# Feed-forward stage on the un-normalized residual, factors applied at eviction; retention scores first; last column's half on VectorE

## The reference

```python
def rms_norm(x, w):
    y = x * lax.rsqrt(jnp.mean(x * x, axis=-1, keepdims=True) + EPS)
    return y * w

h = h + mixed @ w_out                      # 1024 -> 1024
hn = rms_norm(h, ffn_norm_w)
gate, up = jnp.split(hn @ w_gate_up, 2, axis=-1)      # 2 x 2816
h = h + (jax.nn.silu(gate) * up) @ w_down             # 2816 -> 1024
x = rms_norm(h, final_norm_w)
```

## Time and profile before

| | us |
|---|---|
| median of 3 runs | 1132.07 (1131.16 to 1133.46) |
| profiled execution | 1132.3 |
| its span (first to last instruction) | 1130.4 |
| PE busy | 1022.8 (90%) |
| PE loading weights | 712.6 (63%) |
| DVE busy | 845.2 (75%) |
| ACT busy | 423.5 (37%) |
| POOL busy | 305.3 (27%) |
| mean granted clock of TensorE | 0.971 |

### The profile page before, as it was taken

How to read it: one execution, slowest core, us unless ns; L and a number is a source line. 1 busy time by engine, 2 the same in 40 slices (tenths; PEclk the granted TensorE clock), 3 DMA queues, 4 the chain that set the end, 5 groups by cost and what they waited for, 6 DMA issues and landing times.

```text
span 1130.4 us, 14392 instructions
## 1 busy us (share of the span) xinstructions
PE 1022.8 (90%) x5138; PEld 712.6 (63%) x5138; DVE 845.2 (75%) x1758; ACT 423.5 (37%) x842; POOL 305.3 (27%) x288
## 2 busy tenths in 40 slices
PE   7999999999999999999999998878868777777897
PEld 7999999999998877976665554333323333232342
DVE  6979799989778994686796776686776677677555
ACT  7636544354466654352332231221222222122122
POOL 0300000000000000245555534444434444444340
PEclk9999999999999999999999999898989999989899
DMA  9642479898918334599999999999999999999995
GB/s 358 226 149 94 150 281 370 300 333 325 314 55 341 132 115 160 223 420 420 422 420 422 421 422 421 422 422 421 421 422 421 422 420 422 422 421 421 421 422 208
DMA packets 68183, 378.61 MB, mean 335 GB/s; under 512 B 7568, under 2 KB 7952, under 8 KB 35600
## 3 DMA queue, kind: packets, MB, share of 16 engines
q0 software_dynamic: 37152, 268.45, 57.2%
q1 hardware_dynamic: 29808, 106.09, 25.9%
q10 hardware_dynamic: 1152, 3.15, 0.8%
HBM read 376.61 MB, written 1.05 MB: 334 GB/s over the span
## 4 chain that ended last, share of the span: by engine, by line
PE 53%; DMA 32%; DVE 9%; ACT 3%; issue 2%; POOL 1%; POOLq 0%; DVEq 0%; ACTq 0%
DMA ring_sb<-in_peer,idsb 13%; DMA whi_rows<-in_peer,idsb 10%; PE pb L445 9%; PE pb L448 9%; PE pb L954 8%; PE pb L957 7%; PE pb L473 5%; DMA x_rows<-in_peer,idsb 3%; DMA xn<-in_peer,idsb 3%; DMA whi_rows<-in_peer,halves 3%; PE pb L908 2%; PE pb L669 2%; DVE ring_lo L1502 2%; PE pb L894 2%; PE pb L833 1%
## 5 line engine op out<-in xcount | busy, mean ns | idle before, releaser
L2196 DVE CUSTOM_DVE_ANT_0 ring_sb<-ring_sb,arena 128x1024 f32<-128x1024 f32 x127 | 155.2, 1223 | 67.9 <-DMA ring_sb<-in_peer,idsb 67.1
L2319 POOL DMA_INDIRECT ring_sb<-in_peer,idsb x126 | 145.4, 1154 | 144.2 <-PE pb L957 123.5
L445 PE MATMUL pb<-xhi,whi 128*128 128x256 f32 x704 | 178.7, 289 | 4.0 <-DVE arena L1930 2.0
L448 PE MATMUL pb<-xlo,whi 128*128 128x256 f32 x704 | 175.2, 284 | 0.2
L1428 ACT ACTIVATE arena<-arena 128x4 f32<-128x4 f32 (+2 forms) x77 | 15.8, 205 | 425.4 <-DVE arena L2196 425.4
L954 PE MATMUL pb<-ring_sb,arena 128*128 128x512 f32 x254 | 137.5, 624 | 36.2 <-ACT arena L1433 36.2
L2319 POOL DMA_INDIRECT arena<-in_peer,idsb x36 | 40.3, 1119 | 461.3 <-DVE idsb L2087 421.4
L1502 DVE TENSOR_TENSOR ring_lo<-ring_sb,whi 128x1024 fp32r<-128x1024 f32 x126 | 147.8, 1219 | 11.9 <-ACT whi L1017 11.9
L445 PEld LDWEIGHTS pb<-xhi,whi 128*128 128x128 f32 x704 | 135.0, 192 | 7.9 <-issue 2.7
L448 PEld LDWEIGHTS pb<-xlo,whi 128*128 128x128 f32 x704 | 135.0, 192 | 2.4 <-issue 1.4
L957 PE MATMUL pb<-ring_sb,arena 128*128 128x512 f32 x254 | 134.3, 611 | 0.0
(11 more groups left out here) (408 smaller groups left out, 1865.8 us busy)
## 6 DMA issues: line engine op xcount, KB each, us to landing
ring_sb<-in_ada SPq DMA_DIRECT2D x48, 512.0 KB, 5.4
ring_sb<-in_w_gu SPq DMA_DIRECT2D x44, 512.0 KB, 6.9
ring_sb<-in_w_in SPq DMA_DIRECT2D x38, 512.0 KB, 8.2
ring_sb<-in_w_down SPq DMA_DIRECT2D x22, 512.0 KB, 6.0
ring_sb<-in_w_out SPq DMA_DIRECT2D x16, 512.0 KB, 3.5
ring_sb<-in_w_q SPq DMA_DIRECT2D x8, 512.0 KB, 3.9
whi_rows<-in_w_q SPq DMA_DIRECT2D x6, 512.0 KB, 8.7
ring_sb<-in_w_iv SPq DMA_DIRECT2D x4, 512.0 KB, 17.3
```

What stands on the lines that cost most here:

```text
L445: e.matmul(o, hi_w(u)[:, c], xh(k), start=start, stop=False, skip_group_check=skip)
L448: e.matmul(o, hi_w(u)[:, c], xl(k), start=False, stop=False, skip_group_check=skip)
L2196: e.tensor_tensor_reduce(o, o, h2t[tile], 1.0, 0.0, MUL, ADD, aa[:, col:col + 1]).then_inc(*VD.up(("dot", col)))
L2319: e.indirect_dma_start(rows_at[s], None, peer, bass.IndirectOffsetOnAxis(ap=idsb[:, col:col + 1], axis=0)).then_inc(s_row[s], 16)
```

## The change

- *Un-normalized input.* The feed-forward products take h x gain in place of h x gain x rstd. High parts (`ffn_hi`, ScalarE, with the gain as scale) and remainders (`ffn_lo`, VectorE) are written during the output projection, four tiles into places of `xhi`/`xlo` that are free then (`fhi_of(k)` is tile (k+4) mod 8), four after its last product. `normed("n1")` and `x_hi("n1")` go.
- *TensorE's start.* Gate/up 0 is computed in two halves over the feature tiles (`gemm_halves`), with the sums of squares between them and no filler products.
- *Factors at eviction.* In each of the 22 steps VectorE waits for gate/up j and multiplies both halves by the tokens' factors out of PSUM into one SBUF buffer `gus` (`scaled`, 128x512). Sigmoid, silu and glu read `gus`. `sgm` has two buffers in place of four.
- *Order on VectorE.* Within a step the ada parts stand between `scaled` and silu, where they stood behind the rest of glu. The rotary angles move behind the first `scaled`.
- *ScalarE's order.* The two split units that `take` gave at the end of the projection are split behind the last `ffn_hi`, one on each side of `root`/`inv_root`.
- *Scores first.* `scale_x1` moves behind `ret_scores` 0 to 3, and the two group norms behind the scores of their groups.
- *Last column.* For column 255, TensorE adds only the second half of the up row. VectorE adds the first half in `finish`, by a multiplication with the weight and an addition of PSUM.

```diff
+        fhi_of = lambda k: one_(xhi, (k + 4) % 8)
+        flo_of = lambda k: one_(xlo, (k + 4) % 8)
...
-        sgm = [arena[:, i * T:(i + 1) * T] for i in range(4)]
+        gus, sgm = arena[:, 0:2 * T], [arena[:, i * T:(i + 1) * T] for i in (2, 3)]
...
+            def gemm_halves(us, name, until, of, mid):
+                b = bank(until)
+                where[name] = b
+                for h in range(2):
+                    for i, u in enumerate(us):
+                        o = one_(pb[b], i)
+                        if h == 0:
+                            e.wait_ge(*HI.at(u))
+                        for k in range(4 * h, 4 * h + 4):
+                            product(o, u, kc(k), k, fhi_of, flo_of, k == 0 and i == 0, True, (of, k) if i == 0 else False)
+                        if h == 0:
+                            e.wait_ge(*rest_of(u))
+                        for k in range(4 * h, 4 * h + 4):
+                            mm = e.matmul(o, lo_w(u)[:, kc(k)], fhi_of(k), start=False, stop=k == KD - 1, skip_group_check=True)
+                        if h:
+                            mm.then_inc(*USED.up(u))
+                    if h == 0:
+                        mid()
...
-            sums("n1", (4, 10), (AN, ("n1", "ln")))
...
-                gemm([U_gate[j], U_up[j]], ("gu", j), (VG, ("glu", j)), fresh="n1" if j == 0 else None)
+                if j == 0:
+                    gemm_halves([U_gate[0], U_up[0]], ("gu", 0), (VG, ("gu", 0)), "n1", lambda: sums("n1", (0, 0), (AN, ("n1", "ln"))))
+                else:
+                    gemm([U_gate[j], U_up[j]], ("gu", j), (VG, ("gu", j)), xh=fhi_of, xl=flo_of)
...
+                    first_end = end if tile == 0 else col == 254
...
-                    mm = e.matmul(pb[4 + 2 * tile][:, :], dgr[col % 8], o[:, 1024:1536], start=begin, stop=end)
-                    if end:
-                        mm.then_inc(*PU.up(("half", tile)))
+                    if col < 255:
+                        mm = e.matmul(pb[4 + 2 * tile][:, :], dgr[col % 8], o[:, 1024:1536], start=begin, stop=first_end)
+                        if first_end:
+                            mm.then_inc(*PU.up(("half", tile)))
...
+                    if name == "wo":
+                        la.used(2)
+                        if i == 3:
+                            e.wait_ge(*USED.at(us[3][1]))
+                            ffn_hi(4)
+                            ffn_hi(5)
+                        for k in (2 * i, 2 * i + 1):
+                            e.wait_ge(*VN.at((name, k)))
+                            square("n1", k)
+                        if i < 2:
+                            ffn_hi(2 * i)
+                            ffn_hi(2 * i + 1)
+                        if i == 3:
+                            ffn_hi(6)
+                            ffn_hi(7)
+                            rest = new
...
+            def ffn_hi(k):
+                e.activation(fhi_of(k), hk(k), ACT.Copy, scale=vc("ffn", k)).then_inc(*XHI.up(("n1", k)))
...
-            residual(U_wo, "wo", hg_norm)
+            first = residual(U_wo, "wo", hg_norm)
+            split(first[0:1])
             root("n1")
             inv_root("n1")
-            x_hi("n1")
+            split(first[1:2])
...
-                    s = sgm[j % 4]
-                    e.wait_ge(*USED.at(U_up[j]))
-                    if j >= 4:
-                        e.wait_ge(*GLO.at(j - 4))
-                        e.wait_ge(*GHI.at(j - 4))
-                    e.activation(s, one_(pb[where["gu", j]], 0), ACT.Sigmoid).then_inc(*AG.up(("sg", j)))
+                    s = sgm[j % 2]
+                    e.wait_ge(*VG.at(("gu", j)))
+                    if j >= 2:
+                        e.wait_ge(*GLO.at(j - 2))
+                        e.wait_ge(*GHI.at(j - 2))
+                    e.activation(s, one_(gus, 0), ACT.Sigmoid).then_inc(*AG.up(("sg", j)))
...
+                    if name == "wo" and i in (0, 1, 3):
+                        for k in (2 * i, 2 * i + 1) if i < 2 else range(4, 8):
+                            ffn_lo(k)
                     split(la.fill() if i < 2 else new)
+
+            def ffn_lo(k):
+                e.wait_ge(*XHI.at(("n1", k)))
+                e.scalar_tensor_tensor(out=flo_of(k), in0=hk(k), scalar=vc("ffn", k), in1=fhi_of(k).bitcast(F32), op0=MUL,
+                                       op1=SUB).then_inc(*XLO.up(("n1", k)))
...
-            normed("n1", lambda k: vc("ffn", k), one_(rstd, 0))
...
-                    s, b = sgm[j % 4], where["gu", j]
-                    e.wait_ge(*AG.at(("sg", j)))
-                    e.tensor_tensor(s, one_(pb[b], 0), s, MUL).then_inc(*VG.up(("silu", j)))
-                    e.wait_ge(*VG.at(("silu", j)))
-                    e.tensor_tensor(s, s, one_(pb[b], 1), MUL).then_inc(*VG.up(("glu", j)))
-                    e.wait_ge(*GHI.at(j))
-                    e.tensor_tensor(al_of(j), s, ah_of(j).bitcast(F32), SUB).then_inc(*GLO.up(j))
+                    s = sgm[j % 2]
+                    if j == 0:
+                        e.wait_ge(*AN.at(("n1", "rstd")))
+                    e.wait_ge(*USED.at(U_up[j]))
+                    scaled(gus, where["gu", j], VG, ("gu", j))
+                if j == 0:
+                    angles()
                 for n_ in ada_at[j]:
                     if n_ < 46:
                         ada_part(n_)
                     if n_ == 23:
                         turn_32(0)
                         sums_of_32(0)
+                if j < NF:
+                    e.wait_ge(*AG.at(("sg", j)))
+                    e.tensor_tensor(s, one_(gus, 0), s, MUL).then_inc(*VG.up(("silu", j)))
+                    e.wait_ge(*VG.at(("silu", j)))
+                    e.tensor_tensor(s, s, one_(gus, 1), MUL).then_inc(*VG.up(("glu", j)))
+                    e.wait_ge(*GHI.at(j))
+                    e.tensor_tensor(al_of(j), s, ah_of(j).bitcast(F32), SUB).then_inc(*GLO.up(j))
                 if 2 <= j < NF:
                     take([U_dn[j - 2]], 1)
...
-            scale_x1()
...
             for h in range(4):
                 ret_scores(h)
-                if h == 2:
-                    group_rms(("o", 0), vc("sbo"), half(ys, 0))
+            scale_x1()
+            group_rms(("o", 0), vc("sbo"), half(ys, 0))
             take(U_rg[0:2])
-            group_rms(("o", 1), vc("sbo"), half(ys, 1))
             for h in range(4, 8):
                 ret_scores(h)
+            group_rms(("o", 1), vc("sbo"), half(ys, 1))
...
+                    if tile and g == 0:
+                        e.wait_ge(*VD.at(("act", NB - 1)))
+                        e.wait_ge(s_up[1], 16)
+                        e.scalar_tensor_tensor(out=dg[:, gsl], in0=rows_at[row_of[255][0]][:, 1024:1536], scalar=ae[:, 255:256],
+                                               in1=pb[6][:, :], op0=MUL, op1=ADD).then_inc(*VO.up("last row"))
+                        e.wait_ge(*VO.at("last row"))
+                        e.tensor_tensor(dg[:, gsl], dg[:, gsl], g2b[:, gsl], MUL).then_inc(*VO.up((tile, g)))
```

More of the change, by code:

```diff
@@ L469, in gemm @@
                     for k in range(KD):
-                        product(o, u, kc(k), k, hi_of, lo_of, k == 0, False, (paced, k) if paced and i == 0 else False)
+                        product(o, u, kc(k), k, xh, xl, k == 0, False, (paced, k) if paced and i == 0 else False)
                     e.wait_ge(*rest_of(u))
                     for k in range(KD - 1):
-                        e.matmul(o, lo_w(u)[:, kc(k)], hi_of(k), start=False, stop=False)
-                    e.matmul(o, lo_w(u)[:, kc(KD - 1)], hi_of(KD - 1), start=False, stop=True).then_inc(*USED.up(u))
+                        e.matmul(o, lo_w(u)[:, kc(k)], xh(k), start=False, stop=False)
+                    e.matmul(o, lo_w(u)[:, kc(KD - 1)], xh(KD - 1), start=False, stop=True).then_inc(*USED.up(u))
                     if i == 0 and mid is not None:
+                        mid()
[16 more added lines that the diff above has]
+                    if h == 0:
                         mid()
@@ L1058, in residual @@
                     new = la.take(us[3], name == "wo") if i == 3 else []
-                    split(new[0:1])
-                    la.used(2)
-                    for j in range(2):
-                        e.wait_ge(*VN.at((name, 2 * i + j)))
-                        square({"wo": "n1", "wo2": "n3"}[name], 2 * i + j)
-                    split(new[1:])
+                    if name == "wo":
[14 more added lines that the diff above has]
+                            rest = new
+                    else:
+                        split(new[0:1])
+                        la.used(2)
+                        for j in range(2):
+                            e.wait_ge(*VN.at((name, 2 * i + j)))
+                            square("n3", 2 * i + j)
+                        split(new[1:])
                     if i < 2:
                         split(la.fill())
+                return rest if name == "wo" else []
```

(14 more changed lines are left out.)

16 lines of the change are left out of this document (3 added, 13 removed).

## The result

The changed kernel takes 1154.21 us (median of 5 runs, 1153.70 to 1154.91) against 1131.99 us: ratio 1.0197 (95% interval 1.0186 to 1.0208), 22.2 us slower. The prediction was 1149.5 with a range of 1137 to 1156. The profiled execution has a span of 1151.8 us, 21.4 more than before.

A forecast was written before the change was run, and what follows sets the result against it. TensorE bounds the feed-forward stage before the change, VectorE's loop with its wait for ScalarE's split after it. Stage 18.1 + clock 1.7 - scores 2.0 - last column 0.4 = +17.4 us, giving 1149.5 us; range 1137 to 1156.

The forecast's parts named there:

- The pace of the stage: Feed-forward steps: VectorE's loop, waiting for ScalarE's split, takes 8.7 us, 9.9 with three ada parts, above TensorE's 8.64.
- The start: Start of the feed-forward stage: gate/up 0 ends near 138.1, TensorE 4.0 us ahead; silu 0 at 147.1 against 145.96 before.
- I cost them at nothing: Output projection: new high parts and remainders delay splits by about 1 us, which TensorE's work covers, so 0 us.
- The clock: Last down block: half speed for some 3.4 us behind TensorE's standstill, plus 1.7 us (bounds 0 and 1.7).
- Scores first: Retention scores: both TensorE waits for VectorE go, minus 2.0 us (bounds 0 and 2.0).
- Last column: End of the kernel: a shorter VectorE operation replaces the wait for TensorE's last product, minus 0.4 us (bounds 0 and 0.4).
- The cover: Feed-forward stage: two steps of lookahead swallow the delay and TensorE stays the bound; 1125.7 us, chance 0.09.
- VectorE alone sets the pace: Feed-forward stage: remainders find splits ready, loop 8.1 us, no clock loss; some 1137 us, chance 0.14.
- The third rival: Two to four further stretches at half clock where there is no cover, 1.7 us each; 1153 to 1156 us, chance 0.10.
- clock below 1.00 within the stage: Feed-forward stage: a granted clock under 1.00 there was listed as a sign that the prediction is wrong.
- bound of about 3 us: TensorE: the Trainium skill's rule, no idle gaps above about 3 us between bursts, quoted for the clock loss.

## Why the prediction came out as it did

- **The pace of the stage: right.** Silu to silu 8.71 us in steps of two ada parts (predicted 8.7), 9.91 with three (9.9), with the idle time ahead of the remainders released by the split; the odd steps too, 14.97 us for step 9 (15.0), 11.80 for step 13 (11.7), 9.38 for step 15 (9.3). The model, each engine in its program order and one coupling, held over 22 steps: from silu 0 to the last down block 192.2 us where it gave 191.9. That the block stood at 339.01 with the bank mended, to the hundredth of the predicted 339.0, is in part luck: silu 0 was 0.3 early, and the way from there 0.3 longer.
- **The start: wrong.** The step that failed is the sum for the start, which let gate/up 0 follow the projection at once (with "I cost them at nothing" for what was added), and so the claim that TensorE is 4.0 us ahead of before. I had followed what the new operations delay, and not in which PSUM bank gate/up 0 would begin. It waited 2.16 us for VectorE to empty it, and behind that, in this execution, its records came at half speed for some 3 us; silu 0 came at 151.00 in place of 147.1. That is 3.9 of the 4.7 us by which the forecast was short, and 4.0 us came back when the bank alone was changed. Then the lead of 4.0 is there: the rows of gate/up 1 start at 139.62 against 143.96 before, 4.3 earlier, 0.3 of it from the execution's own start.
- **The clock: right in kind, mis-sized in place.** The block took 2.5 us longer, not 1.7. 1.9 of it went when the gap was filled; the remaining 0.6 is VectorE's lateness at the sums: from block to sums it takes 6.4 to 6.5 us in each version at full clock there with the factor multiply, and 5.8 to 5.9 in each without it. The row that I had taken for this term I misread: the last of the two records at 696.94 ended at 697.96, and its bracket says 2.85 us of standstill, not 3.9. That the clock would fall here was not certain: it fell behind the 3.72 us in both traces that have them, and not behind 3.25 us in the old order. That part of the term is luck.
- **Scores first: right.** Predicted -2.0; -1.9 alone by the time (ratio 0.9983), -1.8 in the changed kernel's trace (query stage 23.0 us late, behind sums that are 24.8 late).
- **Last column: right but too small to time.** -0.3 by the trace of its own run, predicted -0.4. Between the query stage and the end the changed kernel won 1.6 us, of which 1.25 lie between the last weight and the first addition (1.97 against 3.22): the edit's 0.3 and 1.0 from a last row already there. Why it had landed earlier stays open, and so do the other 0.35 us.
- **The rivals.** The cover did not hold: TensorE waited for the split in five places, 11.6 us: 3.3 at gate 3 (predicted 3.5), 6.1 behind the transpose, and 0.3 to 1.0 at the others, less than the 1.3 per step that I gave. "VectorE alone sets the pace", priced at 1137, did not happen in the changed kernel. Without the wait for the split (one ada part ahead) it took 1140.85, which is 1136.9 less the 4.0 of the late start, near that price. The third rival's sign came true, a clock below 1.00 within the stage (0.97 over 142 to 318 us; it fell behind the waits of 3.3 and 6.1 us, not behind those near 1), but not its price: there the loop does not wait for TensorE, as I had argued, and with the bank mended the block stood where it was predicted.

A clock below 1.00 within the stage was also on my list of signs of being wrong; it should not have been, since the prediction itself expected such a fall at gate 3, and found it hidden.

In sum, from the trace: +22.3 (last down block) + 2.5 (block) - 1.8 - 1.6 = +21.4, the difference of the spans.

## What to carry to other kernels

When an operation is added to an engine near its limit, write out one full turn of its loop with the waits, not its busy share: 0.60 us of work per step cost as much as it did because 1.0 us of waiting per step was already there or new. Each wait for another engine's short answer (sigmoid, high part, split) needs a piece of independent work directly behind the operation that asks; divide what you have over the places and don't pile it at one. And when a stage is made to start earlier, look up which buffer the turn gives it: here a bank still in use ate the whole head start.

## What the hardware did that I had not expected

- A standstill of TensorE of 2.16 us (131.13 to 133.29) was followed by records 0.21 us apart from 134.0 to 137.2 (granted clock 0.50 over 133.96 to 137.15); I had reckoned with this behind longer gaps only. Of the five traces with this wait three show the fall and two don't, and the 3.25 us in the old order had none behind it. So the bound of about 3 us that the prediction quotes does not sort these cases: the clock fell behind a shorter gap and held behind a longer one.
- Behind the 3.72 us ahead of the last block the records were 0.21 us apart for 5.7 us, more than the 3.4 of the earlier trace rows, which holds full-speed records too.
- The multiplication of 128x512 out of PSUM shows a duration of 0.68 us, and its successor starts 0.60 behind it, as in the earlier trace rows; no form of silu and glu was shorter for reading SBUF: 0.42 in all.
